# The latent layer's attention loop: pair 6 and 7 scored one pair further ahead, the last head projected before pair 3's values, a swap before a slab split

## The reference

```python
q = (rmsnorm(cq, g_q) @ w_uq).reshape(Bn, T, 16, 64 + 32)      # 16 heads
q_nope, q_pe = q[..., :64], rope(q[..., 64:], pos)              # rotated part
kv = (lat_all @ w_ukv).reshape(Bn, L, 16, 64 + 64)              # keys, values
logits = (q_nope @ k_nope.T + q_pe @ kpe_all.T) * scale         # by head
prob = softmax(where(admitted, logits, -inf))
out = (prob @ v).reshape(Bn, T, 16 * 64) @ w_out
```

## Time and profile before

| | |
|---|---|
| median of three runs | 1737.21 us (1733.6 to 1743.05) |
| the profiled execution | 1737.47 us, its span 1735.6 us |
| mean granted clock of TensorE | 0.985 |
| TensorE, matmuls busy | 1653.9 us, 95% |
| VectorE, ScalarE, GpSimd busy | 1150.6, 855.8, 745.6 us |
| latent layer's heads and pairs | about 1020 to 1105 us of the span |

### The profile page before, as it was taken

One profiled execution on the slowest core, in us unless ns is written; L12 is line 12 of the kernel. 1 busy time (PEld: TensorE's weight loads), 2 busy tenths in 40 slices (PEclk: granted clock), 3 DMA queues, 4 the chain that ended last, 5 costly groups with the idle time before them and its releaser, 6 DMA issues.

```text
span 1735.6 us, 37514 instructions
## 1 busy us (share of the span) xinstructions
PE 1653.9 (95%) x14117; PEld 1568.6 (90%) x14117; DVE 1150.6 (66%) x2061; ACT 855.8 (49%) x1604; POOL 745.6 (43%) x815
## 2 busy tenths in 40 slices
PE   6989999996988997999999999999999999999998
PEld 5869999994778997999999887999999977999998
DVE  4686777637478455677764738777774577777753
ACT  3474656433653433365643446366642456566633
POOL 5664666210045210266631437266631765466600
PEclk9999999997999999999999999999999999999999
DMA  7314555453220002455545412355545621555443
GB/s 196 119 41 142 146 148 154 131 148 106 91 97 31 10 5 82 122 146 148 154 131 152 126 58 74 99 159 153 147 123 152 171 85 52 149 154 153 125 138 112
DMA packets 344994, 205.11 MB, mean 118 GB/s; under 512 B 22456, under 2 KB 342312, under 8 KB 344752
## 3 DMA queue, kind: packets, MB, share of 16 engines
q1 hardware_dynamic: 342640, 199.76, 40.2%
q0 software_dynamic: 2080, 3.67, 0.8%
q10 hardware_dynamic: 160, 0.10, 0.0%
HBM read 200.02 MB, written 3.39 MB: 117 GB/s over the span
## 4 chain that ended last, share of the span: by engine, by line
PE 83%; DVE 9%; issue 3%; ACT 3%; POOL 2%; DMA 0%; SPq 0%; DVEq 0%; POOLq 0%; ACTq 0%
PE bank L913 23%; PE bank L914 23%; PE bank L915 23%; PE bank L1301 5%; PE bank L925 1%; DVE lo L2095 1%; ACT hi L1594 1%; DVE SW L2288 1%; PE bank L1240 1%; PE bank L1325 1%; DVE top L2285 1%; PE bank L975 1%; PE bank L1309 1%; POOL qcos L685 1%; DVE xn L2333 0%
## 5 line engine op out<-in xcount | busy, mean ns | idle before, releaser
L913 PE MATMUL bank<-XH,hi 128*128 128x320 f32 (+1 forms) x1976 | 623.1, 315 | 9.7 <-DVE lo L2095 3.2
L2095 DVE TENSOR_TENSOR lo<-raw,hi 128x2048 fp32r<-128x2048 f32 (+4 forms) x197 | 418.7, 2125 | 300.5 <-ACT hi L1594 300.5
L915 PE MATMUL bank<-XH,lo 128*128 128x320 f32 (+1 forms) x1976 | 613.4, 310 | 0.0
L914 PE MATMUL bank<-XL,hi 128*128 128x320 f32 (+1 forms) x1976 | 613.4, 310 | 0.0
L1594 ACT ACTIVATE hi<-raw 128x2048 fp32r<-128x2048 f32 (+4 forms) x205 | 359.9, 1756 | 75.7 <-PE bank L915 63.5
L913 PEld LDWEIGHTS bank<-XH,hi 128*128 128x128 f32 (+1 forms) x1976 | 371.8, 188 | 24.5 <-issue 9.7
L914 PEld LDWEIGHTS bank<-XL,hi 128*128 128x128 f32 (+1 forms) x1976 | 372.2, 188 | 1.6 <-issue 0.4
L915 PEld LDWEIGHTS bank<-XH,lo 128*128 128x128 f32 (+1 forms) x1976 | 371.9, 188 | 0.0
L715 POOL TENSOR_TENSOR upad<-upad,rstd 128x128 f32<-128x128 f32 (+1 forms) x176 | 167.4, 971 | 200.3 <-ACT upad L1675 200.3
L913 PE MATMUL bank<-GH,hi 128*128 128x322 f32 x704 | 219.8, 312 | 0.0
L914 PE MATMUL bank<-GL,hi 128*128 128x322 f32 x704 | 218.7, 311 | 0.0
(11 more groups left out here) (384 smaller groups left out, 2375.5 us busy)
## 6 DMA issues: line engine op xcount, KB each, us to landing
raw<-in_f_w_up SPq DMA_DIRECT2D x176, 512.0 KB, 5.0
raw<-in_f_w_down SPq DMA_DIRECT2D x64, 704.0 KB, 4.7
raw<-in_a_w_in SPq DMA_DIRECT2D x12, 1024.0 KB, 5.2
raw<-in_b_w_rkv SPq DMA_DIRECT2D x12, 1024.0 KB, 5.2
raw<-in_a_w_out SPq DMA_DIRECT2D x8, 1024.0 KB, 5.2
raw<-in_b_w_out SPq DMA_DIRECT2D x4, 1024.0 KB, 5.3
raw<-in_c_w_out SPq DMA_DIRECT2D x4, 1024.0 KB, 5.1
raw<-in_a_w_in SPq DMA_DIRECT2D x12, 256.0 KB, 4.7
```

The source lines that it names most:

```text
L913: pe.matmul(out, a, xh(k), start=(start and k == 0), stop=False)
L914: pe.matmul(out, a, xl(k), start=False, stop=False)
L915: last = pe.matmul(out, b, xh(k), start=False, stop=(stop and k == kt - 1))
L2095: dve.tensor_tensor(lo[n % 2][:, 0:w_], raw[n % 2][:, 0:w_], hi[n % 2][:, 0:w_].bitcast(F32), ALU.subtract).then_inc(w_lo, 1)
```

## The change

No instruction is added or taken away; the order changes on three engines, in layer 2 alone.

- TensorE: head 15 is projected directly behind head 14, ahead of pair 3's values. Pair 6's scores come at the end of turn 3 instead of at the start of turn 4; between the two nothing else stood. Pair 7's scores come in turn 4, behind the turn of pair 4 and ahead of its values, instead of at the start of turn 5.
- ScalarE: heads 14 and 15 are copied behind exps(5) and ahead of out_hi(3). Exps(6) follow out_hi(3), ahead of pt_copy(4). Exps(7) follow out_hi(4), ahead of split_hi of slab s0+10 and of pt_copy(5).
- VectorE: heads 14 and 15 are swapped in turn 3 behind probs(4). Maxima(6) follow out_lo(3), ahead of the split of slab s0+9. Maxima(7) follow probs(5). Ahead of the loop, head 1 is swapped before the split of slab s0+6 and not after it.

```diff
 (pe_mla)
                 for p in range(PAIRS):
-                    if p + 2 < PAIRS:
+                    if p < 4:
                         pair_qk(p + 2)
                     turn_probs(Q + p)
-                    if p + 4 < PAIRS:
+                    if p < 4:
                         project(2 * p + 8)
+                    if p == 3:
+                        project(15)
+                    if p == 4:
+                        pair_qk(7)
...
                     values(Q + p, vals)
-                    if p + 4 < PAIRS:
+                    if p < 3:
                         project(2 * p + 9)
+                    if p == 3:
+                        pair_qk(6)
 (act_mla)
                     pt_copy(Q + p)
-                    if p + 2 < PAIRS:
+                    if p < 4:
                         exps(Q + p + 2)
+                    if p == 3:
+                        head(14)
+                        head(15)
                     out_hi(Q + p, p)
-                    if p + 4 < PAIRS:
+                    if p < 3:
                         head(2 * p + 8)
                         if p in (0, 2):
                             split_hi(s0 + 8 + p // 2)
                         head(2 * p + 9)
+                    if p in (3, 4):
+                        exps(Q + p + 3)
                     if p == 4:
                         split_hi(s0 + 10)
 (dve_mla)
                 head(0)
+                head(1)
                 split_lo(s0 + 6)
-                for h in range(1, 4):
-                    head(h)
+                head(2)
+                head(3)
...
-                    if 2 * p + 7 < 16:
+                    if p < 4:
                         head(2 * p + 6)
                         head(2 * p + 7)
-                    if p + 2 < PAIRS:
                         maxima(Q + p + 2, masks, C_SCALE)
                     pt_copy(Q + p)
                     if p + 1 < PAIRS:
                         probs(Q + p + 1)
+                    if p == 3:
+                        head(14)
+                        head(15)
+                    if p == 4:
+                        maxima(Q + 7, masks, C_SCALE)
                     out_lo(Q + p, p)
+                    if p == 3:
+                        maxima(Q + 6, masks, C_SCALE)
                     if p in (1, 3, 5):
                         split_lo(s0 + 8 + p // 2)
```

## The result

The changed kernel takes 1744.14 us in the median of 17 runs (1739.96 to 1748.29), the kernel before 1738.96 in 17 runs beside it. The ratio is 1.0032, 95% interval 1.0022 to 1.0042: +5.6 us, between 3.8 and 7.3. The medians themselves differ by 5.2 us. The sum of the prediction was +5.4. Its absolute figure, 1742.6, is 1.5 us low, because the three runs that it was built on have a median 1.75 us under that of the 17. The runs resolve more finely than the 0.5% within which the prediction expected the change to stay. It does stay there, and it is slower, by a third of a per cent.

The account below looks back on a forecast made before the run. The prediction took TensorE, busy for 95% of the span, to bound the kernel. Swap +0.1, loop's queues +3.2 and clock +2.1 made +5.4 us, forecast 1742.6 us, range 1735.5 to 1748.

Parts of the forecast that it names:

- Pair 3 and the gain: TensorE, pair 3 onward: qk(6) stays in place, heads 14 and 15 come early, pair 7's scores start 2.5 us sooner.
- What would show it: Signs in the profile after: qk(7) near 1077.9, about 5 us wait ahead of values 5; wrong if pt_copy(5) precedes 1086.
- What takes its place: ScalarE's exps(7) and slab split delay pt_copy(5): 5.1 us hole, values 5 +3.5 us, values 6 +3.2 us.
- The clock: TensorE's granted clock falls behind the 5.1 us hole ahead of values 5: +2.1 us, between nothing and 2.9.
- that case: The forecast with a clock fall: +5.4 us in total, bounds +4.0 and +7.2, chance 0.56.
- B: Rival, loop: queues as forecast but the clock stays at 1.00; +3.3 us, 1740.5 us, chance 0.22.
- The swap: Head 1's swap ahead of the split, before the first scores: GpSimd's next product blocked instead; +0.1 us, bounds 0 and +0.5.
- C: Rival, VectorE and GpSimd: the split takes QT 15's turn, 0.65 us more; +6.0 us with the clock, 1743.2, chance 0.12.
- D: Rival, behind pair 3: the four TensorE holes close and nothing replaces them; −3.8 us, 1733.4, chance 0.06.
- E: Rival, after the loop: a later wait takes up what values 5 lose; +0, 1737.2 us, chance 0.04.

Follow-up runs that it names:

- Clearing ScalarE's queue: Loop's new order with the old first swaps, second output slab's ScalarE split moved before exps(6), exps(7) behind pair 5's output; ratio 1.0004 to the kernel before.
- loop-only: Kernel before with only the loop's new order, first swaps as they were; 1746.72 us, ratio 1.0041 to the kernel before.
- hole filled: Changed kernel plus 30 extra unread matmuls behind pair 5's turn, ahead of its values; ratio 1.0020 to the kernel before, stretch 80.54 us.
- swap-only: Kernel before with only the second head's swap moved ahead of the slab split; 1740.42 us, ratio 1.0004 to the kernel before.
- split earlier: Changed kernel with ScalarE's split of the second output slab moved from turn 4 to turn 3, ahead of exps(6); ratio 1.0021 to the kernel before.
- copies first: Loop-only plus cleared ScalarE queue, pt_copy(4) ahead of exps(6), VectorE's copies for pairs 4 to 7 ahead of slab splits; 1737.04 us, ratio 0.9990 to before.

## Why the prediction was right, and where it was not

**Pair 3 and the gain.** Right. Qk(6) stays in place, heads 14 and 15 come early, and qk(7) starts 8.83 us behind project 14 (1066.40 to 1075.23), where 8.97 was predicted and 11.51 was measured before. The split had a wait of 0.3 us for QT 15, as allowed for. The times under "What would show it" have to be shifted by the 2.48 us: pt_copy(5) starts at 1084.72 in the profile after, which is 1087.2 on the prediction's scale, behind its limit of 1086.

**What takes its place.** Right, as a mechanism and nearly in size. Values 5 come 19.0 us behind project 14, 3.2 us later than before, where +3.5 was predicted; the hole is 4.94 us, not 5.1. Clearing ScalarE's queue took 4.9 us off the loop-only kernel's stretch. With the hole filled against the swap-only kernel the loop costs 80.54 − 77.59 = 2.95 us without its clock, for 3.2 predicted. Of the 0.3 us that values 5 come sooner than predicted, 0.16 is there when exps(7) start (14.31 us behind project 14, for 14.47), and the rest comes by the end of the copy (18.94 for 19.17).

**The clock.** Right for the place: a fall behind the hole in both profiles of the changed kernel, and in loop only and split earlier. Size 2.1 us by the filled hole, as predicted (82.67 − 80.54). The prediction had chosen 2.1 between nothing and 2.9 us, so that it hits to the tenth is luck. In the loop-only kernel it is 4.19 − 2.95 = 1.2 us, so the term varies with how much of the low clock falls into the hole. The lower bound of that case, +4.0, has no working: its own terms give 2.5 us with a fall that costs nothing. B, the case without a fall, is excluded for this order in the profiles taken.

**The swap.** This is the step that failed: "I take +0.1 us there, bounds 0 and +0.5". The prediction let GpSimd's QT 0 run and the split block the next product. GpSimd before, at the product ahead of the split of 1025.79 and at QT 0 behind it:

```profile
1025.32 0.87 POOL L691 TENSOR_TENSOR qsin<-qsin,con 96x320 f32<-96x320 f32 x1
1026.26 2.28 POOL L693 TENSOR_TENSOR QT<-qcos,qsin 96x320 f32<-96x320 f32 x1
```

GpSimd after:

```profile
1022.03 2.81 POOL L693 TENSOR_TENSOR QT<-qcos,qsin 96x320 f32<-96x320 f32 x1
```

and VectorE's split beside it:

```profile
1022.36 1.74 DVE L2106 TENSOR_TENSOR lo<-raw,hi 128x1536 fp32r<-128x1536 f32 x1
```

QT 0 had begun 0.33 us ahead of the split and was held all the same, until 0.74 us behind its end, while the split took 1.74 us, its shortest. So the split blocks the same product as before and not the next one. It starts 0.8 us later, as predicted, and ends 0.52 us later (6.45 us behind the first projection, for 5.93), since before it had itself waited for a product. QT 0 ends later by the same 0.52 us (7.19 for 6.67), and the first scores start 0.5 us later: the upper bound. And the prediction looked for the clock behind the hole that the change makes and not behind the one that it lengthens: with 2.56 us in place of 2.05 a fall there was the rule, for another 1.2 us. The term measured 1.7 us in place of 0.1 against a profile without a fall, and 0.5 + 1.2 x 2/3 = 1.3 if the kernel before has one in one profile of three.

The stretch is then 6.7 us longer, not 5.4: 1.7 for the swap, 2.95 for the loop, 2.1 for the clock. By the means of all profiles, 76.3 before and 82.6 after, it is 6.3. The measured +5.6 (3.8 to 7.3) holds all of these. That the total came within 0.2 us is in part luck: the swap's term was 1.2 to 1.6 us too small, and the timing is not fine enough to show it.

**The rivals.** C, the split taking GpSimd's turn from QT 15, did not come: QT 15 was under way at 1074.32 and the split, dispatched at 1074.76, waited. In all six profiles with the loop's new order and the split on VectorE behind maxima(6), QT 15 led by 0.43 to 0.45 us and the split waited. It was QT 0, which led by 0.33 us, that lost. D was refuted: a gain came only after ScalarE's queue was cleared, and then was 0.7 us of stretch, not 3.8, since holes of 0.90, 0.74 and 1.34 us took the place of the old ones; the last of them is a wait for VectorE's copy. E was refuted by the timing: the interval of +3.8 to +7.3 us excludes zero. In the first profiles 637.8 us lie from the end of the stretch to the last instruction before (1735.6 − 1097.80) and 637.9 after, so nothing takes the loss up there; but the other two profiles of the kernel before have 642.4 and 641.1, so this pair alone would not carry it.

## What to carry to other kernels

When work is moved forward in a hand-written order, list for every engine what it now stands ahead of: here a gain of 2.7 us on TensorE's scores of one pair put exponentials and a slab split ahead of a copy on ScalarE, and that copy released TensorE. Jobs without a near consumer (slab splits) belong behind the small copies that others wait for, or into an idle stretch that the trace shows; here this took the loss away, and whether it makes the kernel faster than before is not shown. Look at TensorE's clock behind each hole that a change makes or lengthens, and take several profiles: a fall costs one to three us, and the kernel before has it in some executions.

## What the runs showed of the hardware

Which of two engines waits when a GpSimd product and a VectorE subtraction meet was not settled by which began first in the profile. A product that had begun 0.33 us ahead of a subtraction was held (2.81 us instead of 0.87; so in seven profiles). With 0.44 us of lead the subtraction was held instead (2.56 us instead of 2.28; so in six). A lead of 0.1 us was enough for that in another place, in the kernel with the copies first, where the subtraction took 2.40 us for 1.74:

```profile
1045.59 0.88 POOL L693 TENSOR_TENSOR QT<-qcos,qsin 96x320 f32<-96x320 f32 x1
```
```profile
1045.69 2.40 DVE L2108 TENSOR_TENSOR lo<-raw,hi 128x1536 fp32r<-128x1536 f32 x1
```

The Trainium skill, "SBUF — State Buffer", section "Who interferes with whom", gives the shared ports to whichever instruction issues first for its whole length. The second and the third meeting agree; the first does not, if the profile's start is the issue. What decided it stays open.

VectorE's scaling of the probabilities took 8.59 us instead of 1.24 beside GpSimd's back-to-back subtractions, which kept their 1.27 us each.

The granted clock fell to 0.50 behind a hole of 2.05 us in two of seven profiles and behind 2.56 us in five of five. It also fell behind holes of 1.37 and 0.96 us, in both profiles of a kernel that differs there from the one before only by a shift of half a us. Useless matmuls in a hole kept the clock up in the place where they stood. They gave 2.1 us in one kernel, but in the other the clock fell later all the same.
